# A decoder trunk: the conditioning units of layer 1 get three buffers of their own and stand in groups of three and two

## The reference, cut to what matters

```python
for l in range(DEPTH):                       # DEPTH = 2
    mod = c_act @ w_ada[l] + b_ada[l]        # 9 x 12288
    sh1, sc1, g1, sh2, sc2, g2 = split(mod, 6)
    hn = rmsnorm(x, norm1_g[l]) * (1 + sc1) + sh1
    m = token_mixers(hn, ...)                # hn @ w_in[l], three head groups, @ w_out[l]
    x = x + g1 * m
    hn = rmsnorm(x, norm2_g[l]) * (1 + sc2) + sh2
    up = hn @ ffn_w_up[l]                    # 2048 x 11264, then a conv of width 3
    x = x + g2 * ((silu(gate) * val) @ ffn_w_down[l])   # 5632 x 2048
y = rmsnorm(x, final_g)
```

## Time and profile before

| | |
|---|---|
| median of 3 runs | 3540.88 us (3539.16 to 3541.62) |
| profiled execution | 3545.56 us, span 3543.8 us, mean granted clock 0.968 |
| TensorE matmul (PE) | busy 3345.6 us, 94% of the span |
| VectorE (DVE) | 1942.5 us, 55% |
| ScalarE (ACT) | 1424.0 us, 40% |
| GpSimd (POOL) | 145.5 us, 4% |
| chain that ended last | PE 87%, DVE 4%, DMA 4% |
| loads of w_ada | 384 of 512 KB, median 4.6 us from issue to landing |
| HBM read | 628.10 MB |

### The profile page before, as it was taken

One profiled execution on the slowest core, in us unless ns is written; L12 is line 12 of the kernel. 1 busy time (PEld: TensorE's weight loads), 2 busy tenths in 40 slices (PEclk: granted clock), 3 DMA queues, 4 the chain that ended last, 5 costly groups with the idle time before them and its releaser, 6 DMA issues.

```text
span 3543.8 us, 58245 instructions
## 1 busy us (share of the span) xinstructions
PE 3345.6 (94%) x23904; PEld 3076.8 (87%) x23904; DVE 1942.5 (55%) x3745; ACT 1424.0 (40%) x2448; POOL 145.5 (4%) x189
## 2 busy tenths in 40 slices
PE   5799999897999999999998999998899999999998
PEld 2588887787999999999998998888899999999997
DVE  0444553657655455545556566546676646665664
ACT  0344333434433333333334553443454434443443
POOL 2000010002000000000001000101100000000001
PEclk7799999998999999999999999999999999999999
DMA  9767666753777767777763444434434444444443
GB/s 315 238 218 221 217 209 208 237 169 122 233 232 235 235 226 230 237 234 232 231 226 123 131 133 117 119 108 155 128 119 152 152 149 149 149 151 147 155 141 113
DMA packets 484122, 646.41 MB, mean 182 GB/s; under 512 B 25742, under 2 KB 427514, under 8 KB 483528
## 3 DMA queue, kind: packets, MB, share of 16 engines
q1 hardware_dynamic: 473472, 608.51, 53.3%
q0 software_dynamic: 10384, 34.17, 3.4%
HBM read 628.10 MB, written 14.49 MB: 181 GB/s over the span
## 4 chain that ended last, share of the span: by engine, by line
PE 87%; DVE 4%; DMA 4%; issue 2%; ACT 2%; DVEq 1%; ACTq 0%; POOL 0%; SPq 0%; POOLq 0%
PE PS L1345 85%; DMA RAW<-in_w_ada 4%; PE PS L1362 1%; PE PS L1349 1%; DVE WLO L921 1%; DVEq L912 1%; ACT WHI L628 0%; DVE CY L1107 0%; DMA RAW<-in_w_in 0%; DVEq L935 0%; DMA KEEP<-in_k_keep 0%; POOL SQ L517 0%; DVEq L915 0%; DVE ST L1084 0%; DVE QP L1127 0%
## 5 line engine op out<-in xcount | busy, mean ns | idle before, releaser
L921 DVE TENSOR_TENSOR WLO<-RAW,WHI 128x512 fp32r<-128x512 f32 x1584 | 1058.1, 691 | 1071.0 <-ACT WHI L628 1051.0
L628 ACT ACTIVATE WHI<-RAW 128x512 fp32r<-128x512 f32 x1584 | 977.3, 629 | 1422.4 <-PE PS L1345 1139.0
L1345 PE MATMUL PS<-HH,WHI 128*128 128x320 f32 (+1 forms) x4384 | 1389.1, 317 | 60.7 <-DVE WLO L921 28.7
L1345 PE MATMUL PS<-HL,WHI 128*128 128x320 f32 (+1 forms) x4384 | 1365.7, 312 | 0.0
L1345 PE MATMUL PS<-HH,WLO 128*128 128x320 f32 (+1 forms) x4384 | 1365.0, 311 | 0.0
L1345 PEld LDWEIGHTS PS<-HH,WHI 128*128 128x128 f32 (+1 forms) x4384 | 826.1, 188 | 126.2 <-issue 84.2
L1345 PEld LDWEIGHTS PS<-HL,WHI 128*128 128x128 f32 (+1 forms) x4384 | 826.3, 188 | 0.0
L1345 PEld LDWEIGHTS PS<-HH,WLO 128*128 128x128 f32 (+1 forms) x4384 | 826.2, 188 | 0.0
L1345 PE MATMUL PS<-MH,WHI 128*128 128x320 f32 x1920 | 605.7, 315 | 41.2 <-DVEq L935 23.7
L1345 PE MATMUL PS<-ML,WHI 128*128 128x320 f32 x1920 | 596.8, 311 | 0.0
L1345 PE MATMUL PS<-MH,WLO 128*128 128x320 f32 x1920 | 596.5, 311 | 0.0
(11 more groups left out here) (274 smaller groups left out, 1727.1 us busy)
## 6 DMA issues: line engine op xcount, KB each, us to landing
RAW<-in_w_ada SPq DMA_DIRECT2D x384, 512.0 KB, 4.6
RAW<-in_ffn_w_up SPq DMA_DIRECT2D x352, 512.0 KB, 3.6
RAW<-in_ffn_w_down SPq DMA_DIRECT2D x176, 512.0 KB, 3.6
RAW<-in_w_in SPq DMA_DIRECT2D x160, 512.0 KB, 3.7
RAW<-in_w_out SPq DMA_DIRECT2D x64, 512.0 KB, 3.6
RAW<-in_w_in SPq DMA_DIRECT2D x32, 384.0 KB, 3.6
ST<-in_state_gla POOLq DMA_DIRECT2D x8, 576.0 KB, 7.0
out_gla_s<-ST POOLq DMA_DIRECT2D x8, 576.0 KB, 4.2
```

The costliest lines, as they stand in the source:

```text
L628: A(WHI[:, g % 4], RAW[:, u % 4, c % 4:c % 4 + 2, :], ACT.Copy).then_inc(hi_ready, 1)
L921: V.tensor_tensor(WLO[:, g % 4], RAW[:, u % 4, c % 4:c % 4 + 2, :], WHI[:, g % 4].bitcast(f32), ALU.subtract).then_inc(split_ready, 1)
L1345: return nc.tensor.matmul(out, w, x, start=start, stop=stop)
```

## The change

The conditioning units beside layer 0's FFN no longer go through RAW. They have a tile of their own, ARAW, with three buffers in region Z (blocks 26 to 35, where NT, OLC and others lie at other times), and three semaphores. `stream()` returns a fifth list, LOADS: the order of SyncE's issues, in which a number is an entry of UNITS and a tuple is an own load. An own load waits until the unit three before it has been used; the first one waits until the norm before the FFN is complete. Own loads stand in the queue where the loads stood before, behind the load of the next W. `ada_unit` reads ARAW where the mark says so. Span s now begins at W 8 + 20 s, with groups of 3, 3, 3, 3, 2 and 2 units behind its numbers 1, 5, 8, 12, 15 and 18, and its turn behind number 19. WAL moves from block 32 to block 46. The A units at the start and beside layer 0's mixer stay as they were.

```diff
--- before.py
+++ after.py
@@ -112,9 +112,21 @@
 
 
 
-    panels, grans, marks = {}, [], []
+
+    panels, grans, marks, loads, own = {}, [], [], [], 0
+
+    def load(a, mark, half, own):
+        marks[mark] += ((own, True) if half else (len(units), False))
+        if half:
+            loads.append(("B",) + a[1:] + (own,))
+        else:
+            loads.append(len(units))
+            units.append(a)
+        return half
+
     units = [("A", 0, k, k + 1) for k in range(KC * FIRST)]
     count, n = len(units), 0
+    loads += range(count)
     for l in range(DEPTH):
         for half, some in enumerate(layer_panels(l)):
 
@@ -124,7 +136,7 @@
                 supers = [((0, 4), 0, (0, 2) * 7 + (2,)), ((0, 5), 16, (0, 2) * 7 + (2,))]
                 supers += [((0, 6 + j), 32 + 13 * j, (0, 2, 2) * 4) for j in range(6)]
             elif half == 1 and l + 1 < DEPTH:
-                supers = [((l + 1, s), 21 * s, (0, 2, 0, 2, 0, 2, 0, 2, 0, 0) * 2) for s in range(SUPERS)]
+                supers = [((l + 1, s), 8 + 20 * s, (0, 3, 0, 0, 0, 3, 0, 0, 3, 0, 0, 0, 3, 0, 0, 2, 0, 0, 2)) for s in range(SUPERS)]
             beside = {}
             for (of, s), first, per in supers:
                 k = 0
@@ -141,9 +153,8 @@
             later = []
             for w, (p, u) in enumerate(order):
                 while later and later[0][0] <= w - AHEAD:
-                    _, a, mark = later.pop(0)
-                    marks[mark] += (len(units),)
-                    units.append(a)
+                    own += load(*later.pop(0)[1:], half, own)
+                loads.append(len(units))
                 units.append(("W", p, u, len(grans) + 2))
                 for c in (4 * u, 4 * u + 2):
                     grans.append((p, c, len(units) - 1))
@@ -154,10 +165,9 @@
                         later.append((w, ("A", of, x, count), len(marks)))
                     marks.append((len(grans), kind, of, x, count))
             for _, a, mark in later:
-                marks[mark] += (len(units),)
-                units.append(a)
+                own += load(a, mark, half, own)
             assert not beside, (l, half, sorted(beside))
-    return panels, grans, units, marks
+    return panels, grans, units, marks, loads
 
 
 def mixer_jobs():
@@ -218,7 +228,7 @@
 def build(nc, I, O):
     f32, f32r, u8 = mybir.dt.float32, mybir.dt.float32r, mybir.dt.uint8
     ACT = mybir.ActivationFunctionType
-    PANEL, GRAN, UNITS, MARKS = stream()
+    PANEL, GRAN, UNITS, MARKS, LOADS = stream()
     JOB = job_table()
     POS = positions(PANEL)
     NG = len(GRAN)
@@ -281,7 +291,7 @@
         STG = at("STG", [P, 7, 128], f32, z_at + 22 * BLK)
         NT = at("NT", [P, 6, T], f32, z_at + 26 * BLK)
         SL = at("SL", [P, W3], f32, z_at + 28 * BLK)[32:64]
-        WAL = at("WAL", [RANK, H * DK], f32, z_at + 32 * BLK)
+        WAL = at("WAL", [RANK, H * DK], f32, z_at + 46 * BLK)
 
         VTM = at("VTM", [P, 3, W3], f32, m_at)
         MSK = at("MSK", [P, 8, 192], f32, m_at)
@@ -330,6 +340,7 @@
         STF = at("STF", [P, 1408], f32, z_at)
         HIST = at("HIST", [P, NB_FF, 16], f32, z_at + 36 * BLK)
         XO = at("XO", [P, GB, 18, 8], f32, z_at + 41 * BLK)
+        ARAW = at("ARAW", [P, 3, ADA_COLS], f32, z_at + 26 * BLK)
         EXT = at("EXT", [P, 4, 338], f32, z_at)
         YC = at("YC", [P, 4, 338], f32, z_at + 5 * BLK)
         HF = at("HF", [P, 2, T], f32, z_at + 10 * BLK)
@@ -343,6 +354,7 @@
             return ctx.enter_context(nc.semaphore(name))
 
         raw_loaded = [sem(f"raw_loaded{i}") for i in range(4)]
+        own_loaded = [sem(f"own_loaded{i}") for i in range(3)]
         ada_used = sem("ada_used")
         rows_ready = sem("rows_ready")
         mod_done = sem("mod_done")
@@ -461,7 +473,17 @@
 
         @block.sync
         def _(sp):
-            for i, (kind, a, b, value) in enumerate(UNITS):
+            for i in LOADS:
+                if type(i) is tuple:
+                    _, a, b, value, j = i
+                    if j == 0:
+                        sp.wait_ge(hn_ready, 32 * a)
+                    else:
+                        sp.wait_ge(ada_used, value - 3)
+                    row, col = a * D + P * (b % KC), ADA_COLS * (b // KC)
+                    sp.dma_start(ARAW[:, j % 3, :], w_ada[row:row + P, col:col + ADA_COLS]).then_inc(own_loaded[j % 3], 16)
+                    continue
+                kind, a, b, value = UNITS[i]
                 if i >= 4:
                     was, _, _, freed_at = UNITS[i - 4]
                     if was == "A":
@@ -1362,9 +1384,14 @@
                     op = nc.tensor.transpose(out, src, IDENT[row:end, row:end])
                 op.then_inc(job_done, 1)
 
-            def ada_unit(u, b, k):
-                pe.wait_ge(raw_loaded[u % 4], 16 * (u // 4 + 1))
-                w = RAW[:, u % 4].rearrange("p c n -> p (c n)").rearrange("p (b j n) -> p b j n", b=2, j=4)
+            def ada_unit(u, own, b, k):
+                if own:
+                    pe.wait_ge(own_loaded[u % 3], 16 * (u // 3 + 1))
+                    w = ARAW[:, u % 3, :]
+                else:
+                    pe.wait_ge(raw_loaded[u % 4], 16 * (u // 4 + 1))
+                    w = RAW[:, u % 4].rearrange("p c n -> p (c n)")
+                w = w.rearrange("p (b j n) -> p b j n", b=2, j=4)
                 for j in range(4):
                     op = mm(PS[32 * j:32 * j + 32, b, 0:256].rearrange("p (b n) -> p b n", b=2),
                             CACT[:, k, :], w[:, :, j, :], k == 0, k == KC - 1)
@@ -1379,10 +1406,10 @@
                 while marks[0] < len(MARKS) and MARKS[marks[0]][0] <= to:
                     _, kind, _, x = MARKS[marks[0]][:4]
                     if kind == "A":
-                        u = MARKS[marks[0]][5]
+                        u, own = MARKS[marks[0]][5:7]
                         if x % KC == 0 and turned[0]:
                             pe.wait_ge(mod_free, turned[0])
-                        ada_unit(u, 7, x % KC)
+                        ada_unit(u, own, 7, x % KC)
                     else:
                         turned[0] += 1
                         pe.wait_ge(rows_ready, FIRST + turned[0])
@@ -1687,7 +1714,7 @@
             pe.wait_ge(c_ready, 1)
 
             for u in range(KC * FIRST):
-                ada_unit(u, u // KC, u % KC)
+                ada_unit(u, False, u // KC, u % KC)
                 i = (u - 12) // 2
                 if u % 2 or i < 0:
                     continue
```

## The result

The changed kernel takes 3536.44 us (median of 22 runs, 3529.26 to 3543.60) against 3544.24 us of the kernel before (22 runs, 3538.73 to 3549.69). The ratio is 0.9979, with a 95% interval of 0.9972 to 0.9985: 7.4 us less, 5.3 to 9.9. Forecast were 7.7 us less. The forecast time, 3533.2, was set on the three runs of before that were known then (3540.88); with more runs that median lies 3.4 us higher, and so, by 3.2 us, does this one. It is inside the 3530 to 3539 that were given 8 chances in 10, and 0.4 us above the forecast's own range, 3531 to 3536, which hung on the same three runs. That the time shrank is clear of noise; its interval is too wide to tell 7.7 us from the 9.3 of the first rival. The profile does that.

What follows compares the result with a forecast made beforehand. TensorE, busy all the time in layer 0's FFN, was taken as the bound. Fewer groups gave -8.1 us, lost neighbours +0.4, together -7.7 from 3540.88: 3533.2 us, own range 3531 to 3536, 8 in 10 for 3530 to 3539.

Steps and rivals of the forecast that it cites:

- the first rival: Layer 0's FFN, behind W 241: the triple fills the stall too, 9.3 us gained, 3531.6 us; chance 0.07.
- The term that carries the sum: Layer 0's FFN on TensorE: 24 groups fewer at a fixed 0.34 us each, 8.1 us removed.
- The neighbours' term: At W 7, 242, 248 and 251 groups or turns no longer stand beside transposes: 0.11 us each, +0.4 us.
- The supply: SyncE's in-order queue: a triple's last load may take 11 us to land and needs 8.1; cost 0.
- The start: First weight units of layer 0's FFN: W 4 starts 2.4 us earlier with 0.8 us slack; cost 0, at most 2.
- The turn: A turn follows its last group after one W instead of three; cost 0, bound 3.6 us.
- The stall: The 2.1 us wait behind W 241 stays, its chain starting after W 241; gain 0, bound 1.6 us.
- The second: Part of the gain is given back at the norm or by late turns, 3535 to 3538 us; chance 0.10.
- the third: No gain: the price goes with the unit, or a third unit brings its own edge, 3541.3 us; chance 0.06.
- The fourth: Slower: SyncE's in-order queue holds three loads, then bursts; 15 us slower at 1 us each, 3556 us; chance 0.07.

Runs made afterwards that it cites:

- Pairs: The changed kernel with its own buffers and spans of 20, but units in pairs again (96 groups); ratio to the kernel before 0.9995.
- singles: The changed kernel with every conditioning unit alone, 192 groups instead of 72; 3571.72 us, ratio to the kernel before 1.0078.
- 5, 5, 6: The changed kernel with three groups of 5, 5 and 6 units a span, 36 groups, partly through the ring; 3519.82 us, ratio to the kernel before 0.9930.
- the second profile: The changed kernel measured again with nothing altered, beside the kernel before; FFN section 1052.51 us, ratio 0.9968.
- two places later: The changed kernel with its own loads two places later in the queue; one run, 3539.03 us.
- the version with the group moved: The changed kernel with one triple of the last span moved from behind W 240 to behind W 241; ratio to the kernel before 0.9976.
- the loads four places later: The changed kernel with its own loads four places later in the queue; one run, 4070.03 us.

## Why the prediction was right

The term that carries the sum, 24 groups less at a fixed price of 0.34 us, is right, and it is measured apart now. Pairs to singles give 0.33 us a group, pairs to the changed groups (1059.15 + 1.19 - 1052.51) / 24 = 0.33, the changed groups to 5, 5, 6 give 11.7 / 36 = 0.32, with the clock at the section's start made equal 0.34. Two readings need no correction for clock or stall. The first is from turn to turn, with twenty W and no slow step between: kernels with 16, 8, 6, 4 and 3 groups a span take 83.00, 80.39, 79.74, 79.08 and 78.73 us, 0.33 a group over the whole range. The second is the group itself, counted as for the pair in the earlier trace rows: 0.77, 1.20, 1.63, 2.06, 2.49 and 2.93 us for sizes 1 to 6, which is 0.33 + 0.43 a unit.

The Trainium skill has the rule that a change of tiling mode drains TensorE (TensorEngine Tiling (Array Packing), Key Properties). It gives no price and doesn't speak of a group's size. That the price comes once a group, at six sizes, agrees with it, and the estimate with the warm constant of TensorE: Matmul & The Clock Gate was 2 x 0.166 = 0.33 us a group. But a group changes the data type and the operands together with the tiling, and no run tells these apart; the transposes, which stay at 128x128, are followed by a slow step too (0.23 us, 1834.21 to 1834.44 in the changed kernel). So the price for each group is shown, and that it is a drain for the tiling is not.

The neighbours' term was too large: 0.28 us, and not 0.4. At W 248 a pair beside transposes saves the 0.10 that the earlier trace rows show, but at W 7, W 242 and W 251 only 0.05 each. In the sections it can't be told apart: of the 7.85 us between before and the second profile 0.4 are three slow steps fewer at the start, which leaves 7.5, where 24 x 0.33 - 0.3 = 7.6 were due. The supply cost nothing, as forecast: own loads landed in 3.6 to 7.7 us (median 4.8) where 11 were allowed, and even two places later nothing waited. The start cost nothing: no wait between 862 and 1826 us. The turn cost nothing, though a turn now follows its group after one W: no idle time before any of the 48 turn matmuls. The stall stayed at 2.15 us, and the reason given (the chain starts at the end of W 241) was confirmed by moving the group one place.

Of the rivals, the first is excluded for the change as it is (the stall is whole), and shown for the version with the group moved. The second and the third are excluded by the timelines and by the singles. The fourth is a real mechanism: it is priced by the loads four places later. It doesn't set in, since the queue comes to the loads early enough. What the prediction had wrong is at the side: the neighbours' price; the level of the time, which it built on three runs; and the clock behind the stall, which it took as given and which moves a single profile by 1.5 us. The expectations of later runs left the half clock out of the price of a wait and the ring's slots out of a filling.

What the change says of itself is half of the matter. The buffers alone are worth nothing that can be seen here; the groups alone bring it nearly all in the old ring.

## What to carry to other kernels

When the bound engine is busy all the time, look for what it pays per switch between two kinds of work, read from the distance of starts at both edges for two sizes, and make fewer and larger groups; here each switch into 128x32 float32 matmuls and back cost 0.33 us, and going from 96 to 36 groups brought 20 us of 3540 in that section. Buffers follow from the group's size and aren't a gain of their own. Before work is put into a stall, follow the chain that ends the stall and ask what the moved work holds up in every queue it passes.

## What the runs showed of the hardware

A stall of 2.15 us on TensorE, after hundreds of microseconds without one, is followed by the half clock (1.2 GHz) in some executions of the same kernel and not in others: in layer 0's FFN in two of the eight profiles with a stall of 2.15 us or more, in layer 1's in eight of thirteen. In layer 0's two cases it set in at the restart or 0.8 us later, 3.4 us of work ran at half speed, and 1.5 and 1.6 us were lost. At the section's start, behind the norm's 8.3 us of waiting, 11 to 20 steps are slow, another microsecond of scatter from profile to profile. Differences below 2 us between two profiles of this kernel have to be read with the clock beside them.
